# A gated-delta-rule layer: VectorE's gated product and low half queued later, and one dense quarter moved behind the solve's first products

## The chip, the cores and the metric

The kernel runs on one core of one Trainium2 chip. The metric is the device time of one execution in microseconds (us); less is better. A core has TensorE (PE: matrix products into PSUM banks), VectorE (DVE), ScalarE (ACT), GpSimd (POOL) and SyncE (SP), which issues the transfers from HBM. Each engine works through its own list of instructions in order, and waits on semaphores that the others raise.

## What is computed

Two blocks of two layers each run on a sequence of 512 tokens with 1024 features. The change lies in one of the four: the first layer of the second block, a gated delta rule (GDN) with 8 query/key heads and 16 value heads of 128 features. Cut to what matters:

```python
def gated_delta_rule(q, k, v, g, beta):          # chunks of 64 tokens
    L = jnp.where(strict, einsum('bhncd,bhnsd->bhncs', kb, k) * decay, 0.0)
    T = triangular_solve(eye + L, eye, lower=True, unit_diagonal=True)
    u = T @ vb
    w = T @ (kb * exp(g))
    ...
    def step(state, inp):
        v_new = u_n - w_n @ state
        o = q_n @ state + a_n @ v_new
        state = state * gl_n + k_n.T @ v_new
...
o = rmsnorm(o, norm_w) * silu(z)
return o.reshape(B, S, GDN_V_WIDTH) @ w_out
```

The projection before (q, k, v, z) and the one behind (`w_out`) are dense products with 1024 and 2048 rows; `T` is the inverse that the text calls the solve.

## The kernel before

All products are in fp32 precision, made of three products of high and low halves: a weight block (128 x 1024) is loaded as `w_raw`, ScalarE copies its high half (`w_hi`, L261), VectorE subtracts to get the low half (`w_lo`, L267), and PE multiplies hi by hi, hi by lo and lo by hi (L281). The same is done with the layer's output before `w_out`: `o_hi` by ScalarE (L2819), `o_lo` by VectorE (L3020).

The GDN layer works through its 8 query/key heads in 8 turns, of kinds "first" (turn 0), "mid" (turns 1 to 6) and "last" (turn 7). Turn j solves and scans head j, projects q, k, v0 and v1 of head j + 1 and z0 and z1 of its own, and multiplies the gated output of head p = j - 1 by its rows of `w_out` (output tiles `O0` to `O7`). The first turn has no p, and the last has no next head, so it projects only z0 and z1.

The order on every engine is written out by hand. On PE, `turn` alternates a small step of the solve or the scan with dense work named in the table `GDN_BESIDE`: `beside("inv")` issues the units listed at "inv", and so on. A unit such as `v02` is one dense quarter: part 2 of the projection v0, six products of 128 x 512. A unit such as `O0` is one output tile, also six products; the first one, `O0`, waits for `lo_1`, the last piece of `o_lo`.

The steps around the change, in PE's order, each followed by its dense work:

- "inv": while VectorE eliminates 16 by 16 blocks (`ta`, `tb`, 15 pairs of small instructions, then `P` and `PT`), PE has only dense quarters.
- `halves("f")` and `halves("g")` need `PT`; then the dense work of "c".
- `halves("f2")` needs `fb` (ScalarE) and `gb` (VectorE); then "f2".
- `halves("v")` needs `f2a` (ScalarE) and `f2b` (VectorE, L3096); then "v".
- `halves("y")` needs `vb` (VectorE) and `c` (ScalarE); then "y"; then `halves("at")`.

All five are issued at L2495. VectorE's order before the change, from `PT`: one `w_lo`; the convolution of the next q (`conv(0, ...)`, three instructions at L2973); `gated` (two instructions at L3015, `sq * zs`, 128 x 512); `ga` and `gb` (L3092); `ha` and `hb` (L3030); `f2b` (L3096); one `w_lo`; `low` (two instructions at L3020, which wait for `o_hi`); `va` and `vb` (L3030); one `w_lo`; and the convolutions of k and v. The last turn has the same order without the convolutions. Its dense work is `O0` beside "v" and `O1` beside "y", and nothing at "c" and "f2".

ScalarE makes `o_hi` in `high(p)`, behind its copies for `f2a` and `c`, and it waits for `gated` there.

Of the kernel before, what the change touches and what calls it, by code (L numbers as in the profile page):

```python
# [117 lines left out]
def first_and_second_block(nc, a, out):  # L118

    with ExitStack() as ctx:  # L120
# [20 lines left out]
        def tile(name, k, n=1, dt=F32):  # L141

            assert k + n <= 48
            return nc.alloc_sbuf_tensor_at(name, [P, n * T], dt, offset=arena + k * T * 4)
# [1224 lines left out]
        class Gla:  # L1369
            b0, t0 = BASE["gla"]  # L1370
            a_lr = tile("gla_a_lr", 8)
            q, k, v, g = ([gla_qkvg[:, n * T:n * T + T] for n in range(n0, n1)] for n0, n1 in ((0, 2), (2, 4), (4, 8), (8, 12)))
# [458 lines left out]
        class Dsa:  # L1831
            b0, t0 = BASE["dsa"]
            kk, wi, qi = tile("dsa_kk", 8), tile("dsa_wi", 9), [tile(f"dsa_qi{m}", 10 + m) for m in range(2)]
            q, k, v = ([dsa_qkv[:, n * T:n * T + T] for n in range(n0, n1)] for n0, n1 in ((2, 10), (0, 2), (10, 12)))
# [9 lines left out]
            p, pT = [tile(f"dsa_p{m}", 8 + m) for m in range(4)], [tile("dsa_pT0", 45), sumsq]  # L1844
# [441 lines left out]
        class Gdn:  # L2286
# [10 lines left out]
            _, inv, tmp = (gdn_blocks[:, k * P:k * P + P].rearrange("p (i c) -> p i c", i=INV_BLOCK) for k in range(3))  # L2297
# [21 lines left out]
        class GdnAt:  # L2319
# [19 lines left out]
            def through(self, n, i):  # L2339
# [4 lines left out]
        GDN_BESIDE = {  # L2344
# [60 lines left out]
        def gdn_gate(at, i, h):  # L2405

            t = at.t - 2 + h
            return (block_done, SPLIT + at.b - 1 + h + i * 16), bank[t % BANKS], (tile_free, BANKS + t + i * 28), (tile_free, BANKS + t + 1 + i * 28)
# [5 lines left out]
        def first(h):  # L2414
            return bank[(4, 7)[h]]

        def second(h):
            return bank[(5, 6)[h]]
# [505 lines left out]
        def gdn_dve(dve):  # L2924
# [18 lines left out]
            def split(at, i, n):  # L2943
                split_lo(dve, at.block[n] + AHEAD, i, 16)

            p = GDN_QK - 1
# [19 lines left out]
            def conv(u, j, i, at, odd):  # L2966
                dve.wait_ge(*at.through(GDN_CONV[u], i))
                dve.wait_ge(*N.act.after(f"cw{u}", j))
                c, src = gdn_conv(u, odd), at.bank(GDN_CONV[u])
                for d, n in ((1, "a"), (2, "b"), (3, None)):  # L2970
                    if d > 1:
                        dve.wait_ge(*N.dve.after(f"c{'ab'[d - 2]}{u}", j))
                    ins = dve.scalar_tensor_tensor(c[:, d:T], src[:, 0:T - d], par[:, gdn_tap(3 - d, u, j)], c[:, d:T], ALU.mult, ALU.add)  # L2973
                    if n:
                        ins.then_inc(*N.dve.done(f"c{n}{u}"))
                    else:
                        ins.then_inc(tile_free, 1)
# [33 lines left out]
            def gated(p, gates):  # L3011
                for h in range(2):
                    dve.wait_ge(*GdnOut.dve.after(f"on_{h}", p))
                    dve.wait_ge(*gates[h])
                    dve.tensor_tensor(G.sq[h][:], G.sq[h][:], G.zs[h][:], ALU.mult).then_inc(*GdnOut.dve.done(f"o_{h}"))  # L3015

            def low(p):
                for h in range(2):
                    dve.wait_ge(*GdnOut.act.after(f"hi_{h}", p))
                    dve.tensor_tensor(G.o_lo[h][:], G.sq[h][:], G.o_hi[h][:].bitcast(F32), ALU.subtract).then_inc(*GdnOut.dve.done(f"lo_{h}"))  # L3020

            def turn(j, p, i, at):
# [3 lines left out]
                def done(step):  # L3026
                    return H.dve.done(step)

                def tt(step, out, x, y, op):
                    dve.tensor_tensor(out, x, y, op).then_inc(*done(step))  # L3030

                def splits(point):
                    for n in GDN_LOWS[at.kind].get(point, "").split():
                        split(at, i, n)
# [44 lines left out]
                def halves(x):  # L3079
                    return x.rearrange("p (c x) -> p c x", x=INV_PART)  # L3080

                def eye(r):
                    return ident[r, r].rearrange("p (c x) -> p c x", c=1).to_broadcast([P // 2, 2 * TT, INV_PART])
                if more:
                    if p is not None:
                        dve.wait_ge(*gdn_gate(at, i, 1)[3])
                    conv(0, j + 1, i, at, odd)
                if p is not None:
                    gated(p, [gdn_gate(at, i, h)[3] for h in range(2)])
                pe("g")  # L3090
                for n, r, src in (("ga", a, second(0)), ("gb", b, second(1))):
                    dve.tensor_copy(G.m[r, :], src[r]).then_inc(*done(n))  # L3092
                for n, r, src in (("ha", a, second(0)), ("hb", b, second(1))):
                    tt(n, halves(G.V1[r, :]), halves(src[r]), eye(r), ALU.add)
                pe("f2")
                dve.tensor_copy(G.F2[b, :], first(1)[b]).then_inc(*done("f2b"))  # L3096
                splits("vc")
                if p is not None:
                    low(p)
                pe("v")  # L3100
                own("hb")
                for n, r, src in (("va", a, second(0)), ("vb", b, second(1))):
                    tt(n, G.V[r, :], G.V1[r, :], src[r], ALU.add)
                splits("f")
                if more:
                    conv(1, j + 1, i, at, odd)
# [10 lines left out]
                for t in range(TT):  # L3117
# [28 lines left out]
                    splits(f"vn{t}")  # L3146
                splits("end")
            gdn_turns(dve, turn)
            share_low(1)
            scaled_share(0)  # L3150
# [64 lines left out]
        class Fox:  # L3215
# [4 lines left out]
            q2, q3, k2, k3 = ([tile(f"fox_{n}_{h}", 8 + 2 * k + h, dt=F32R) for h in range(2)] for k, n in enumerate(("q2", "q3", "k2", "k3")))  # L3220
            q, k, v = (tile(f"fox_{n}", 16 + t) for t, n in enumerate(("q", "k", "v")))
# [3 lines left out]
            gated = tile("fox_gated", 46)  # L3225
# [557 lines left out]
        y_T, y = tile("y_T", 8, KT), tile("y", 30, KT)  # L3783
# [193 lines left out]
```

## Time and profile before

| | |
|---|---|
| median of 3 runs | 2736.06 us (2734.93 to 2736.99) |
| the profiled execution, whole time | 2736.56 us |
| its span, first to last instruction | 2734.8 us |
| granted TensorE clock, mean | 0.998 of full speed |
| PE busy | 2681.2 us (98%) |
| VectorE busy | 1787.3 us (65%) |
| ScalarE busy | 1274.7 us (47%) |
| GpSimd busy | 899.6 us (33%) |
| six mid turns of the GDN layer | from about 1928 to 2340 us, 68.7 us each |
| the last turn | from about 2335 to 2390 us |

Busy times are shares of the span. A PE that is busy 98% of it leaves few gaps, and it is the gaps on PE that a change of order can close or open. The granted clock is the share of full speed that the throttle let through.

### The profile page before, as it was taken

How to read it: one execution, taken by the hardware profiler on the slowest of the kernel's cores; microseconds unless marked ns; L12 is line 12 of the kernel's file. 1: busy time of each engine (PE TensorE's matmuls, PEld its weight loads, DVE VectorE, ACT ScalarE, POOL GpSimd, SP SyncE). 2: the span in 40 equal slices, each digit the busy share in tenths (PEclk: the TensorE clock that was granted, in tenths of full speed). 3: DMA queues.
4: the chain of work that ended last, by engine and by line, in shares of the span. 5: the costliest groups of instructions: out<-in, count | busy, mean ns of one | idle time of the engine just before them, and what ended most of it. 6: DMA issues, size and time to landing. Idle time of an engine off the chain costs nothing.

```text
span 2734.8 us, 40987 instructions
## 1 busy us (share of the span) xinstructions
PE 2681.2 (98%) x15550; PEld 2223.8 (81%) x15550; DVE 1787.3 (65%) x2641; ACT 1274.7 (47%) x2008; POOL 899.6 (33%) x751
## 2 busy tenths in 40 slices
PE   8999999999999999999999999999999999899998
PEld 6998888789888898887788998877777777777777
DVE  7974336569753687635956887348777777676664
ACT  4542232445323453223554543345555555467775
POOL 5520013136431264403733545104422222122232
PEclk9999999999999999999999999999999999999999
DMA  5343332223553325533213256322222222122222
GB/s 144 87 123 93 96 82 78 82 80 101 170 159 94 96 85 157 175 96 85 78 31 90 83 145 181 106 70 71 78 70 70 70 70 63 44 78 65 66 62 70
DMA packets 484876, 255.94 MB, mean 94 GB/s; under 512 B 17843, under 2 KB 478422, under 8 KB 484710
## 3 DMA queue, kind: packets, MB, share of 16 engines
q1 hardware_dynamic: 484534, 253.40, 32.4%
q8 instruction: 111, 1.82, 0.3%
q14 instruction: 55, 0.45, 0.1%
q10 hardware_dynamic: 176, 0.27, 0.0%
HBM read 251.51 MB, written 2.13 MB: 93 GB/s over the span
## 4 chain that ended last, share of the span: by engine, by line
PE 89%; DVE 6%; ACT 2%; issue 1%; POOL 1%; DMA 0%; SPq 0%; DVEq 0%; ACTq 0%; POOLq 0%
PE bank L281 60%; PE bank L978 12%; PE bank L2495 1%; PE bank L2526 1%; PE bank L2528 1%; DVE w_lo L267 1%; PE bank L2527 1%; DVE dsa_work L2191 1%; PE bank L3435 1%; PE bank L3427 1%; DVE small L2185 1%; PE bank L2640 1%; PE bank L3460 1%; DVE gdn_blocks L3030 1%; PE bank L1569 1%
## 5 line engine op out<-in xcount | busy, mean ns | idle before, releaser
L267 DVE TENSOR_TENSOR w_lo<-w_raw,w_hi 128x1024 fp32r<-128x1024 f32 x365 | 463.1, 1271 | 463.2 <-ACT w_hi L261 443.8
L281 PE MATMUL bank<-x_hi,w_hi 128*128 128x512 f32 x1808 | 737.7, 408 | 6.0 <-DVE w_lo L267 4.2
L281 PE MATMUL bank<-x_lo,w_hi 128*128 128x512 f32 x1808 | 707.8, 391 | 0.6 <-DVE x_lo L623 0.6
L281 PE MATMUL bank<-x_hi,w_lo 128*128 128x512 f32 x1808 | 707.5, 391 | 0.0
L261 ACT ACTIVATE w_hi<-w_raw 128x1024 fp32r<-128x1024 f32 x349 | 366.9, 1056 | 489.7 <-PE bank L281 440.7
L281 PEld LDWEIGHTS bank<-x_hi,w_hi 128*128 128x128 f32 x1808 | 340.4, 188 | 88.1 <-issue 16.5
L281 PEld LDWEIGHTS bank<-x_hi,w_lo 128*128 128x128 f32 x1808 | 340.1, 188 | 74.3
L281 PEld LDWEIGHTS bank<-x_lo,w_hi 128*128 128x128 f32 x1808 | 341.1, 189 | 68.1 <-DVE x_lo L623 3.9
L468 POOL TENSOR_TENSOR sumsq<-sumsq,sq 128x512 f32<-128x512 f32 x56 | 90.3, 1613 | 711.8 <-ACT sq L456 711.2
L281 PE MATMUL bank<-h_hi,w_hi 128*128 128x512 f32 x768 | 300.3, 391 | 0.0
L281 PE MATMUL bank<-h_hi,w_lo 128*128 128x512 f32 x768 | 299.0, 389 | 0.0
L281 PE MATMUL bank<-h_lo,w_hi 128*128 128x512 f32 x768 | 298.8, 389 | 0.0
L281 PEld LDWEIGHTS bank<-h_hi,w_hi 128*128 128x128 f32 x768 | 144.2, 188 | 30.6
L281 PEld LDWEIGHTS bank<-h_hi,w_lo 128*128 128x128 f32 x768 | 144.2, 188 | 30.5
L281 PEld LDWEIGHTS bank<-h_lo,w_hi 128*128 128x128 f32 x768 | 144.2, 188 | 29.4
L978 PE MATMUL bank<-t_hi,w_hi 128*128 128x256 f32 x512 | 146.1, 285 | 0.7 <-DVE w_lo L1192 0.7
L978 PE MATMUL bank<-t_lo,w_hi 128*128 128x256 f32 x512 | 144.8, 283 | 0.0
L978 PE MATMUL bank<-t_hi,w_lo 128*128 128x256 f32 x512 | 144.8, 283 | 0.0
L716 POOL TENSOR_TENSOR sumsq<-sumsq,ada_hi 128x512 f32<-128x512 f32 x48 | 62.1, 1293 | 160.9 <-DVE ada_hi L702 160.9
L978 PE MATMUL bank<-x_hi,w_hi 128*128 128x256 f32 x384 | 109.2, 284 | 0.3
L978 PE MATMUL bank<-x_lo,w_hi 128*128 128x256 f32 x384 | 108.7, 283 | 0.0
L978 PE MATMUL bank<-x_hi,w_lo 128*128 128x256 f32 x384 | 108.6, 283 | 0.0
(542 smaller groups left out, 5070.1 us busy)
## 6 DMA issues: line engine op xcount, KB each, us to landing
w_raw<-in_ffn_wi_dram SPq DMA_DIRECT2D x176, 512.0 KB, 3.8
w_raw<-in_ffn_wo_dram SPq DMA_DIRECT2D x64, 512.0 KB, 3.5
w_raw<-in_ada_w_dram SPq DMA_DIRECT2D x48, 512.0 KB, 4.8
w_raw<-in_a_w_in_dram SPq DMA_DIRECT2D x48, 512.0 KB, 4.0
w_raw<-in_b_w_in_dram SPq DMA_DIRECT2D x32, 512.0 KB, 4.0
w_raw<-in_ffn_wo_dram SPq DMA_DIRECT2D x32, 384.0 KB, 3.1
w_raw<-in_even_w_in_dram SPq DMA_DIRECT2D x16, 512.0 KB, 4.0
w_raw<-in_a_w_out_dram SPq DMA_DIRECT2D x16, 512.0 KB, 3.5
```

What stands on the lines that cost most here:

```text
L261: act.activation(w_hi[b % SPLIT][:], w_raw[raw % RAW][:], ACT.Copy).then_inc(w_hi_done, 1)
L267: dve.tensor_tensor(w_lo[s][:], w_raw[raw_of(b) % RAW][:], w_hi[s][:].bitcast(F32), ALU.subtract).then_inc(w_lo_done, 1)
L281: mm = pe.matmul(out, lhs[:, w], rhs(kt), start=first and kk == 0 and m == 0, stop=last and kk == len(kts) - 1 and m == 2)
L468: pool.tensor_tensor(sumsq[:], sumsq[:], sq[k % 2][:], ALU.add).then_inc(sum_added, 1)
L716: pool.tensor_tensor(dst, x, y, ALU.add).then_inc(ada_added, 1)
L978: mm = pe.matmul(out, lhs[:, w], rhs[:, k, :], start=first and k == 0 and m == 0, stop=k == 3 and m == 2, skip_group_check=True)
L1569: pe.matmul(out[:], w_hi[b % SPLIT][:, w], h_hi[:, x], start=first and kt == kts[0], stop=False)
L2185: dve.max(S.top8, w).then_inc(*s.done(f"top{t}_{k}"))
L2191: dve.match_replace(w, S.top8, w, TAKEN).then_inc(*s.done(f"out{t}_{k}"))
L2495: mm = pe.matmul(out[:, c * INV_PART:(c + 1) * INV_PART], lhs(c), rhs(c), start=True, stop=True)
L2526: pe.matmul(out[:], w_hi[s][:, x], G.o_hi[h][:], start=h == 0, stop=False)
L2527: pe.matmul(out[:], w_hi[s][:, x], G.o_lo[h][:], start=False, stop=False)
```

## The change

Two things are moved and nothing is added or taken away. In the table for mid turns, the dense quarter `v02` goes from "inv" (in front of `f` and `g`) to "c" (behind them, in front of `f2`). In VectorE's turn, of every kind that has a p, `gated` goes from in front of `ga` to behind `hb`, and `low` goes from in front of `va` to behind `vb`.

```diff
-            "mid": {... "inv": "k0 k1 k2 k3 v00 v01 v02", "c": "v03", "f2": "v10", "v": "v11 v12", "y": "v13 O0",
+            "mid": {... "inv": "k0 k1 k2 k3 v00 v01", "c": "v02 v03", "f2": "v10", "v": "v11 v12", "y": "v13 O0",
...
                     conv(0, j + 1, i, at, odd)
-                if p is not None:
-                    gated(p, [gdn_gate(at, i, h)[3] for h in range(2)])
                 pe("g")
                 for n, r, src in (("ga", a, second(0)), ("gb", b, second(1))):
                     dve.tensor_copy(G.m[r, :], src[r]).then_inc(*done(n))
                 for n, r, src in (("ha", a, second(0)), ("hb", b, second(1))):
                     tt(n, halves(G.V1[r, :]), halves(src[r]), eye(r), ALU.add)
+                if p is not None:
+                    gated(p, [gdn_gate(at, i, h)[3] for h in range(2)])
                 pe("f2")
                 dve.tensor_copy(G.F2[b, :], first(1)[b]).then_inc(*done("f2b"))
                 splits("vc")
-                if p is not None:
-                    low(p)
                 pe("v")
                 own("hb")
                 for n, r, src in (("va", a, second(0)), ("vb", b, second(1))):
                     tt(n, G.V[r, :], G.V1[r, :], src[r], ALU.add)
+                if p is not None:
+                    low(p)
                 splits("f")
```

## Rows read from the trace of the kernel before

**Rows 1.** The page: the chain that ended last, by engine.

```profile
PE 89%; DVE 6%; ACT 2%; issue 1%; POOL 1%; DMA 0%; SPq 0%; DVEq 0%; ACTq 0%; POOLq 0%
```

**Rows 2.** Busy time of each engine over six windows, one per mid turn: sum.

```profile
sum 412.00, PE 402.57 PEld 326.66 DVE 300.63 ACT 226.74 POOL 120.33; mean PE 67.10 PEld 54.44 DVE 50.11 ACT 37.79 POOL 20.06
```

**Rows 3.** PE's waits, 1890 to 2400 us: total, times, longest (us).

```profile
PE bank L2495 <- issue: 7.6, 6, 1.6
PE bank L2495 <- DVE gdn_W L3030: 1.8, 6, 0.3
```

**Rows 4.** The chain of waits in one mid turn: start, length (us).

```profile
2002.38 9.74 PE bank L281 x42
...
2014.14 1.59 PE bank L281 x6
```

**Rows 5.** PE's timeline, same turn: start, length; in brackets the idle before.

```profile
2012.06 1.15 PE L2495 MATMUL bank<-gdn_E,gdn_P 64*64 64x64 f32 x32
...
2014.07 0.50 PE L281 MATMUL bank<-x_hi,w_hi 128*128 128x512 f32 x1
...
2016.93 0.27 PE L2495 MATMUL bank<-gdn_W,gdn_W 64*64 64x64 f32 x2 [1.20 <-issue]
...
2019.61 1.15 PE L2495 MATMUL bank<-gdn_W,gdn_W 64*64 64x64 f32 x32
2020.69 0.50 PE L281 MATMUL bank<-x_hi,w_hi 128*128 128x512 f32 x1
...
2024.01 0.24 PE L2495 MATMUL bank<-gdn_W,gdn_W 64*64 64x64 f32 x1 [0.31 <-DVE gdn_W L3030]
```

**Rows 6.** VectorE's timeline in the same turn.

```profile
2010.27 0.71 DVE L3076 STREAM_TRANSPOSE gdn_P<-gdn_P 128x512 f32<-128x512 f32 x1
...
2012.01 2.31 DVE L2973 SCALAR_TENSOR_TENSOR gdn_qT<-bank,par,gdn_qT 128x511 f32<-128x511 f32 x3
2014.23 1.28 DVE L3015 TENSOR_TENSOR gdn_sq<-gdn_sq,gdn_zs 128x512 f32<-128x512 f32 x2
2015.43 1.40 DVE L3092 COPY gdn_W<-bank 64x512 f32<-64x512 f32 x2
2016.87 1.41 DVE L3030 TENSOR_TENSOR gdn_W<-bank,ident 64x512 f32<-64x512 f32 x2
2018.19 0.69 DVE L3096 COPY gdn_W<-bank 64x512 f32<-64x512 f32 x1
2018.91 1.23 DVE L267 TENSOR_TENSOR w_lo<-w_raw,w_hi 128x1024 fp32r<-128x1024 f32 x1
2021.13 1.29 DVE L3020 TENSOR_TENSOR gdn_o_lo<-gdn_sq,gdn_o_hi 128x512 fp32r<-128x512 f32 x2 [1.00 <-ACT gdn_o_hi L2819]
2022.46 1.40 DVE L3030 TENSOR_TENSOR gdn_W<-gdn_W,bank 64x512 f32<-64x512 f32 x2
```

**Rows 7.** PE's timeline in the last turn.

```profile
2358.22 0.27 PE L2495 MATMUL bank<-gdn_W,gdn_W 64*64 64x64 f32 x2 [1.55 <-DVE gdn_W L3092]
...
2360.27 1.15 PE L2495 MATMUL bank<-gdn_W,gdn_W 64*64 64x64 f32 x32 [0.89 <-DVE gdn_W L3096]
2362.58 0.47 PE L2526 MATMUL bank<-gdn_o_hi,w_hi 128*128 128x512 f32 x1 [1.16 <-issue]
...
2364.14 0.27 PE L2495 MATMUL bank<-gdn_W,gdn_W 64*64 64x64 f32 x1
```

**Rows 8.** VectorE's timeline in the last turn.

```profile
2359.48 0.69 DVE L3096 COPY gdn_W<-bank 64x512 f32<-64x512 f32 x1
2361.19 1.29 DVE L3020 TENSOR_TENSOR gdn_o_lo<-gdn_sq,gdn_o_hi 128x512 fp32r<-128x512 f32 x2 [1.02 <-ACT gdn_o_hi L2819]
```

**Rows 9.** PE's timeline in the first turn.

```profile
1885.70 1.40 PE L2495 MATMUL bank<-gdn_E,gdn_P 64*64 64x64 f32 x32 [2.15 <-DVE gdn_P L3076]
```

**Rows 10.** Busy time and PE clock, two windows, first and last turn.

```profile
1885.70:1890.00 4.30, 4.30 (x67) 3.98 (x68) 3.11 (x5) 2.24 (x3) 4.30 (x4) 0.60 0.02 4
...
2354.00:2360.00 6.00, 3.24 (x112) 3.02 (x112) 5.91 (x9) 2.81 (x4) 0.00 (x0) 1.00 0.33 90
```

2 rows, old and new, of the table GDN_BESIDE are left out of this document.

## The prediction

> **What bounds the kernel now.** I read the page first. The chain that ended last runs on PE for 89% and on VectorE for 6% [rows 1], so a change of order is worth only the PE gaps that it closes, less those that it opens. The edit touches the GDN layer alone, so I took busy time by turn next. In six mid turns, 412.00 us, PE is busy 402.57 [rows 2]: some 1.6 us of gap in a turn of 68.7. PE's waits over the layer name them [rows 3]: six gaps in front of the small products at L2495 put down to "issue", 7.6 us in all, and six for VectorE at L3030, 1.8 us. One of each falls in every mid turn, and the two timelines of one turn show which they are.
>
> The "issue" gap is that of `f2` at 2016.93 [rows 5]. The product waits for `gb`, which ends at 2015.43 + 1.40 = 2016.83, 0.10 before it [rows 6]; so the gap is a wait for VectorE, although the view does not name one. The other, 0.31, is in front of `y` at 2024.01, behind `vb`, which ends at 2022.46 + 1.40 = 2023.86. VectorE works without a pause from `PT` to the `w_lo` at 2018.91 [rows 6]. What stands between `PT` and `gb` there includes `gated`, which PE does not need until much later.
>
> **The change in a mid turn, step by step**, in the times of this turn.
>
> - `f` and `g`. They need `PT`, which ends at 2010.27 + 0.71 = 2010.98 [rows 6], and started at 2012.06, so PE now has about 1.1 us of cover. A dense quarter in that run takes 9.74 / 7 = 1.39 [rows 4]. Without `v02`, PE would be there at 2010.67, before `PT`; with 0.15 from the end of a VectorE result to the product (2023.86 to 2024.01), `f` starts at 2011.13. A wait of about 0.45 is new here.
> - "c". `f` and `g` take 2014.07 - 2012.06 = 2.01 [rows 5], so the dense work starts at 2013.14. One quarter there takes 1.59 [rows 4], a second one 1.39: 2.98. PE is ready for `f2` at 2016.12.
> - `gb`. `gated` gave VectorE 2015.43 - 2014.23 = 1.20 of work in front of it. Now `ga` starts at 2014.23 (`g` is over by about 2013.3), and `gb` ends at 2014.23 + 1.40 = 2015.63. This is before 2016.12: the gap of 1.20 is closed, and `f2` starts 0.81 earlier.
> - `f2b`. The same instructions stand before it, `gated` now behind `hb`, so it still ends at 2018.19 + 0.69 = 2018.88. `f2` and the quarter behind it take 2019.61 - 2016.93 = 2.68, and PE is ready for `v` at 2018.80. With 0.10 of delay `v` starts at 2018.98: a wait of 0.18 is new, and `v` is 0.63 earlier than before. VectorE, not PE, now sets this point.
> - `y`. `v` takes 2020.69 - 2019.61 = 1.08, two quarters 2.98: PE is ready at 2018.98 + 4.06 = 2023.04. The results of `v` reach VectorE at about 2018.98 + 1.2 = 2020.2; the `w_lo` is done at 2020.14, and `va` and `vb` follow without `low` in front: `vb` ends at 2021.6. The gap of 0.31 is closed. `y` starts 0.97 earlier.
> - `low`. It runs from 2021.6 to 2022.9; even the `o_hi` of before was there by 2021.13 [rows 6]. `gated`, which `o_hi` waits for, ends at 2018.2 instead of 2015.5, still 2.9 in front of that, so I count nothing for it. `O0` reads `lo_1` behind `y` and one quarter, at 2023.04 + 1.08 + 1.59 = 2025.7, with 2.8 us in hand; if that cover were gone, each microsecond would count in full.
> - The rest. From `vb` on VectorE is about 1.1 ahead of its old times, PE 0.97. The `w_lo` pieces, the convolutions and the chain of the scan follow the one or the other, and so does GpSimd, which waits for `vb`. Block v0 ends some 0.4 later than before on PE, long before ScalarE and VectorE convolve it. No transfer is moved: SP's order is untouched, and its loads wait for `w_lo` pieces which come no later.
>
> Six mid turns: 6 x 0.97 = 5.8 us gained. A lower bound is 0.63 per turn (3.8), if the second gap does not close.
>
> **The first turn** has no p, and its table is not changed: nothing.
>
> **The last turn** has no convolution and little dense work, and takes the same order on VectorE. Before it, `ga` followed `g` almost at once, with `gated` hidden in the wait for `g`; so `f2`, at 2358.22 behind `gb` [rows 7], gains nothing. `gated` now delays `f2b` by 1.20: its end goes from 2359.48 + 0.69 = 2360.17 [rows 8] to 2361.37, and `v` starts at 2361.47. The results of `v` come at 2362.67, `va` and `vb` take 1.40 to 2364.07, and then `low` takes 1.29 to about 2365.3. But `O0`, the dense work beside "v", waits for `lo_1`: before, it started at 2362.58, 0.10 behind `low` [rows 7, 8]. Now it starts at 2365.4, with `va`, `vb` and `low` all in front of it and PE idle, and `y` stands behind `O0` on PE. `y` and all that follows are 2.8 us later; nothing in this turn can give it back, as what follows is a chain paced by PE and by its own results.
>
> **The clock.** PE would be idle from about 2359.4 to 2365.4 but for 1.15 us of `v`. In the first turn, after an idle of 2.15 us [rows 9], the granted clock fell shortly after the small products began, and the 4.30 us behind were run at a mean of 0.60 [rows 10]: its lower level, 1.2 GHz, for most of it. That is 4.30 x 0.40 = 1.7 us of work at full speed lost. In the last turn of before, PE was busy 3.24 of 6.00 us and the clock stayed at 1.00 [rows 10]. Now the pauses are 2.1 and 2.8 us, so a fall is likely. Its price lies between nothing (it falls and is released inside the pause) and 1.7; I take 1.3, nearer the upper end, since the dense work starts directly behind the pause.
>
> The Trainium skill (TensorE: Matmul & The Clock Gate, "What's actually happening") has it that half rate is the default and that activity releases it. By that rule the work behind the pauses starts at half rate; by the last turn of before alone it would stay at full speed, and the kernel would be 1.3 us faster than I forecast. The trace agrees with the rule in the first turn, with the 0.60 above.
>
> **The sum.** -5.8 + 2.8 + 1.3 = -1.7 us. The profiled execution took 2736.56 us (span 2734.8 and 1.8 around it), 0.5 above the median of the runs, so I take the difference alone to the median: 2736.06 - 1.7 = 2734.4 us.
>
> **The rivals.**
>
> - The clock holds in the last turn: -5.8 + 2.8 = -3.0, 2733.1 us. For it: it held there before. Against it: [rows 9, 10]. Chance 0.22.
> - The mid turns don't keep their gain: some other chain (ScalarE's roots, VectorE's elimination in the next turn) is the true pace, and only the last turn's loss is seen: +2.8 + 1.3 = +4.1, 2740.2 us, slower. Its place is the new wait in front of `f`: if it grows until it eats the gain. For it: VectorE is the last to come at `f` and at `v` after the change. Against it: from PE's sums of one turn to the elimination of the next, VectorE's work starts from PE's own result, so it moves with PE, and I have counted that wait (0.45). It decides the sign where the gain of a turn is below 4.1 / 6 = 0.68. Chance 0.1, of which 0.04 for a loss over 0.2%.
> - The last turn loses nothing, as `low` and `O0` find cover that I don't see: -5.8, 2730.3 us. Against it: `O0` waits for `lo_1` already now. Chance 0.06.
> - The change does nothing, both edits cancelling in every turn: 2736 us. It would need `f` to wait 1.4 rather than 0.45. Chance 0.04.
>
> My forecast has 0.58.
>
> **How the numbers follow.** A change of 0.2%, 5.5 us, is about what a measurement of this kernel can tell from none. My forecast, the clock's rival and most of the second one lie inside. Beyond -5.5 lies only the rival of the last turn, at its edge: faster 0.05. Beyond +5.5 only a second rival with a further loss: slower 0.04. The range runs from 2731.2, the upper bound of the gain with part of the last turn's loss, to 2737.6, the lower bound of the gain (3.8), 2.8 and a clock fallen in full (1.7), which is +0.7, and the spread of the runs of before (1 us either way).
>
> **What the changed profile would show.** In a mid turn: `f2` with no gap in front, a gap of 0.4 to 0.5 in front of `f` and one of about 0.2 in front of `v` released by L3096, none in front of `y`; six windows of 67.7 us instead of 68.7. In the last turn: `v` 1.2 later behind `f2`, a pause of about 2.8 in front of `O0`, and a granted clock under 1.00 around it. I am wrong if mid turns stay at 68.7, or if `O0` starts right behind `v` there.

## The result and the profile after

The changed kernel takes 2746.77 us (median of 6 runs, 2745.87 to 2748.40) against 2736.30 us of the kernel before (6 runs): a ratio of 1.0039, 95% interval 1.0027 to 1.0051. It is 10.5 us slower. I had forecast 2734.4, 1.7 us faster, and given a loss of over 0.2% a chance of 0.04.

The profiled execution took 2745.87 us, with a span of 2744.1 (before 2734.8), 9.3 us longer. The start of `PT` (L3076) in each turn divides it. From turn 1 to turn 7 it is 2357.5 - 1939.6 = 417.9 us, against 2353.7 - 1941.6 = 412.1: six mid turns of 69.65 us instead of 68.68, +5.8. From `PT` of the last turn to the copy of T (L3109) it is 19.9 us against 14.3: +5.6. From the first turn's `PT` to turn 1 it is 55.3 against 56.8, and `PT` of the first turn came 0.5 earlier: together 2.0 us less, which has nothing to do with the edit. In the profiled execution of before the granted clock fell in the first turn [rows 9, 10], and in this one it did not; over all profiled executions of this study that stretch takes 56.7 or 56.8 us where the clock falls in it and 55.3 where it does not. What follows the copy of T is 0.1 shorter: 5.8 + 5.6 - 2.0 - 0.1 = 9.3. Through the six mid turns the granted clock is 1.00 in both executions, so their 5.8 us are not the clock's.

PE's waits over the mid turns of the changed kernel (us in total, times, longest):

```profile
PE bank L2635 <- DVE gdn_W L3141: 5.1, 6, 0.9
PE bank L2495 <- DVE gdn_P L3076: 2.6, 6, 0.8
PE bank L2495 <- issue: 2.3, 6, 0.4
PE bank L2526 <- DVE gdn_kT L2973: 1.8, 6, 0.3
PE bank L2640 <- ACT gdn_T L2826: 1.2, 6, 0.2
```

They answer to [rows 3]. The gaps in front of `f2` (7.6) and `y` (1.8) are gone, and the waits that I had foreseen are there: `f` behind L3076, 0.4 a turn, and `v`, 0.4 ("issue"). Three more are new, all behind VectorE's work after `vb`: an output tile waits for the convolution of k, the scan for `ct` (a copy by ScalarE, which had itself waited for that convolution), and the first product of the scan's second step (L2635) 0.9 us for VectorE's copy of the state.

VectorE's timeline of one mid turn from `ga` on, in the changed kernel, which answers to [rows 6]:

```profile
2083.05 1.40 DVE L3090 COPY gdn_W<-bank 64x512 f32<-64x512 f32 x2
2084.47 1.41 DVE L3030 TENSOR_TENSOR gdn_W<-bank,ident 64x512 f32<-64x512 f32 x2
2085.91 1.29 DVE L3015 TENSOR_TENSOR gdn_sq<-gdn_sq,gdn_zs 128x512 f32<-128x512 f32 x2
2087.24 0.69 DVE L3096 COPY gdn_W<-bank 64x512 f32<-64x512 f32 x1
2087.96 1.23 DVE L267 TENSOR_TENSOR w_lo<-w_raw,w_hi 128x1024 fp32r<-128x1024 f32 x1
2089.22 1.41 DVE L3030 TENSOR_TENSOR gdn_W<-gdn_W,bank 64x512 f32<-64x512 f32 x2
2090.66 0.69 DVE L3020 TENSOR_TENSOR gdn_o_lo<-gdn_sq,gdn_o_hi 128x512 fp32r<-128x512 f32 x1
...
2091.26 1.77 DVE L3020 TENSOR_TENSOR gdn_o_lo<-gdn_sq,gdn_o_hi 128x512 fp32r<-128x512 f32 x1
2092.96 2.31 DVE L267 TENSOR_TENSOR w_lo<-w_raw,w_hi 128x1024 fp32r<-128x1024 f32 x1
2095.30 2.32 DVE L2973 SCALAR_TENSOR_TENSOR gdn_kT<-bank,par,gdn_kT 128x511 f32<-128x511 f32 x3
```

Down to `vb` it is as forecast. Then the second piece of `low` takes 1.77 us instead of 0.69, and the `w_lo` behind it 2.31 instead of 1.23, with the same shapes: 2.2 us in which VectorE is busy by the profile and late for everything behind. GpSimd's timeline of the same stretch, in the changed kernel; `da` (L3171) and `db` (L3174), two instructions each, make the decay matrices of the next head from inputs in SBUF:

```profile
2090.70 1.78 POOL L3171 TENSOR_TENSOR gdn_dec<-gdn_gb,not_above 128x512 f32<-128x512 f32 x1 [24.54 <-DVE gdn_W L3030]
...
2092.45 1.73 POOL L3171 TENSOR_TENSOR gdn_dec<-gdn_gb,not_above 128x512 f32<-128x512 f32 x1
2094.15 2.02 POOL L3174 TENSOR_TENSOR gdn_dec<-gdn_dec,gdn_cols 128x512 f32<-128x512 f32 x1
```

GpSimd waits for `vb` and starts `da` at 2090.70, 0.04 behind the first piece of `low`. From there the two engines take turns. `low`'s second piece ends 0.55 behind the end of the first `da` (2092.48), the `w_lo` 1.1 behind the end of the second `da` (2094.18), 0.14 less than each takes alone, and each GpSimd instruction is in turn longer by what VectorE does first. In the kernel before, GpSimd started with the `w_lo` at 2023.89, and this is its row:

```profile
2023.94 2.32 POOL L3171 TENSOR_TENSOR gdn_dec<-gdn_gb,not_above 128x512 f32<-128x512 f32 x1 [26.57 <-DVE gdn_W L3030]
```

There GpSimd paid (2.32 us), and VectorE did not (1.23): it was 0.05 ahead, and the convolutions that followed, which take one input from PSUM, ran at their usual 2.31 beside `da` and `db`. The edit put `low`, two instructions with both inputs in SBUF, between `vb` and the `w_lo`. Only the first instruction of such a run has the lead.

The last turn of the changed kernel, on PE (answers to [rows 7]), and the clock of a stretch of it:

```profile
2362.03 0.27 PE L2495 MATMUL bank<-gdn_W,gdn_W 64*64 64x64 f32 x2 [1.55 <-DVE gdn_W L3090]
2365.52 1.97 PE L2495 MATMUL bank<-gdn_W,gdn_W 64*64 64x64 f32 x32 [2.33 <-DVE gdn_W L3096]
2370.35 0.77 PE L2526 MATMUL bank<-gdn_o_hi,w_hi 128*128 128x512 f32 x1 [2.86 <-issue]
```

```profile
2364.00:2373.00 9.00, 4.62 (x38) 3.63 (x38) 5.18 (x8) 2.42 (x4) 0.00 (x0) 0.50 0.02 4
```

The two pauses, 2.33 and 2.86 us, are where the prediction had them, and the granted clock is 0.50, its lower level of 1.2 GHz, for the 9 us of this window. It fell inside the first pause, at 2363.7; `v` took 1.97 us instead of 1.15 [rows 7].

### The profile page after: what moved, and what is told of

It reads as the page before. It is cut to its first block, busy times and chain, and to the rows that moved or that the text cites. A ratio compares the mean times of both kernels' runs of the same rounds, so it can differ in the third digit from the quotient of the medians.

```text
span 2744.1 us, 40987 instructions
## 1 busy us (share of the span) xinstructions
PE 2683.8 (98%) x15550; PEld 2224.5 (81%) x15550; DVE 1803.4 (66%) x2641; ACT 1274.8 (46%) x2008; POOL 904.4 (33%) x751
## 3 DMA queue, kind: packets, MB, share of 16 engines
q8 instruction: 111, 1.82, 0.3%
## 4 chain that ended last, share of the span: by engine, by line
PE 84%; DVE 12%; issue 2%; ACT 1%; POOL 1%; DMA 0%; DVEq 0%; SPq 0%; ACTq 0%; POOLq 0%
PE bank L281 57%; PE bank L978 12%; DVE w_lo L267 2%; DVE gdn_blocks L3030 2%; PE bank L2495 1%; DVE gdn_vT L2973 1%; DVE dsa_work L2191 1%; DVE small L2185 1%; PE bank L3435 1%; PE bank L3427 1%; PE bank L2526 1%; PE bank L3460 1%; PE bank L2528 1%; PE bank L1569 1%; PE bank L2527 1%
## 5 line engine op out<-in xcount | busy, mean ns | idle before, releaser
L267 DVE TENSOR_TENSOR w_lo<-w_raw,w_hi 128x1024 fp32r<-128x1024 f32 x365 | 472.2, 1298 | 461.1 <-ACT w_hi L261 441.9
```

The lines of the kernel that those rows point to most:

```text
L267: dve.tensor_tensor(w_lo[s][:], w_raw[raw_of(b) % RAW][:], w_hi[s][:].bitcast(F32), ALU.subtract).then_inc(w_lo_done, 1)
```

## The experiments

The port theory, formed from these rows: a VectorE instruction with both inputs in SBUF and a GpSimd instruction can't run at once, so `low` and the `w_lo` wait for `da`. Rivals: the moved quarter and its waits in front of `f` and `v` cost the time; or the new order costs it by itself, without GpSimd. All ratios are to runs of the kernel before on the same chip.

**GpSimd later, all else as changed** (`dve` is GpSimd's wait for a step of VectorE; `s0_1`, a step of the scan, comes some 14 us behind `vb`).

```diff
-                    dve("PT" if p is None else "vb")
+                    dve("PT" if p is None else "s0_1")
                     front(j + 1, 1 - gdn_odd(at))
```

> The changed kernel in full, but GpSimd begins its work for the next head (the decay rows, da and db) behind s0_1 instead of behind vb. Port theory: VectorE's two pieces of o_lo and the w_lo behind them are held up in the changed kernel by GpSimd's da and db, which start with them; with GpSimd out of the way they take 1.3 and 1.2 us again instead of 2.4 and 2.3, a mid turn takes 67.9 us, and the kernel is 0 to 2 us slower than before (six turns at -0.8, last turn at +5.5). Rival (the moved quarter or the order itself costs the time, not GpSimd): mid turns stay at 69.7 and the kernel stays 10 us slower.

Measured: 2736.55 us, ratio 1.0004 (0.9995 to 1.0013). All pieces of `low` are short again (least, median and longest, ns; before them the changed kernel's row):

```profile
L3020 DVE TENSOR_TENSOR gdn_o_lo<-gdn_sq,gdn_o_hi x14: 684/694/1776, 1951.2 to 2369.6; 128x512 fp32r<-128x512 f32 x14
```

```profile
L3020 DVE TENSOR_TENSOR gdn_o_lo<-gdn_sq,gdn_o_hi x14: 682/688/692, 1951.0 to 2358.8; 128x512 fp32r<-128x512 f32 x14
```

`w_lo` is at 1.21, and six mid turns take 2346.8 - 1939.4 = 407.4, 67.90 each. The order on VectorE and PE is that of the changed kernel; so the loss in the mid turns is GpSimd's overlap, and both rivals fall.

**GpSimd alone, in the kernel before.**

```diff
-                    dve("PT" if p is None else "vb")
+                    dve("PT" if p is None else "s0_1")
```

> The kernel before with GpSimd's da and db behind s0_1, nothing else. Port theory: in the old order only the w_lo behind vb runs beside them, and it was not held up (1.23 us), so a mid turn stays at 68.7 and there is no difference. Rival (GpSimd's place gains by itself, and the run with the full change and GpSimd later was fast for that): 0.8 us per turn less.

Measured: 2736.79 us, 1.0002 (0.9993 to 1.0011), mid turns at 68.70. The place of GpSimd's work is worth nothing until something of VectorE's collides with it.

**GpSimd earlier, in the kernel before.**

```diff
-                    dve("PT" if p is None else "vb")
+                    dve("PT" if p is None else "hb")
```

> The kernel before with one edit: GpSimd begins da and db behind hb instead of behind vb, so that they run beside f2b, the w_lo and o_lo, in the old order on both engines. Port theory: the w_lo behind f2b and the o_lo pieces go from 1.23 and 1.29 us to above 2, vb and y come 1 to 2 us later, and the kernel is 5 to 12 us slower. Rival (only the order of the change costs): no difference.

Measured: 2749.63 us (5 runs), 1.0053 (1.0039 to 1.0067), a mid turn at 71.15: 13 us slower, a little over the upper end expected. Not all of that is GpSimd's overlap. The wait in front of `y` goes from 0.31 to 1.75 us, and in four of the six mid turns the granted clock falls soon behind it. Here is a mid turn without the fall, the next one, with it, and the stretch of the fall:

```profile
2012.34:2082.57 70.23, 67.27 (x566) 54.56 (x565) 52.21 (x95) 37.80 (x61) 20.95 (x17) 1.00 0.24 68
2082.57:2154.37 71.80, 68.84 (x566) 55.70 (x565) 52.31 (x95) 37.90 (x61) 20.95 (x17) 0.98 0.23 67
2099.40:2102.70 3.30, 3.30 (x9) 2.60 (x8) 3.16 (x6) 2.07 (x5) 0.00 (x0) 0.50 0.61 159
```

The overlap costs 1.5 us of a turn (70.2 against 68.7), some 9 us in six, which is within what was expected; the half clock costs another 1.5 in a turn in which it falls. VectorE's timeline of the second of these turns, ahead of the fall at 2099.4:

```profile
2090.49 0.69 DVE L3096 COPY gdn_W<-bank 64x512 f32<-64x512 f32 x1
2091.21 1.82 DVE L267 TENSOR_TENSOR w_lo<-w_raw,w_hi 128x1024 fp32r<-128x1024 f32 x1
2093.44 2.74 DVE L3020 TENSOR_TENSOR gdn_o_lo<-gdn_sq,gdn_o_hi 128x512 fp32r<-128x512 f32 x2 [0.41 <-ACT gdn_o_hi L2819]
2096.21 1.40 DVE L3030 TENSOR_TENSOR gdn_W<-gdn_W,bank 64x512 f32<-64x512 f32 x2
```

The same two kinds are held up, `w_lo` 1.82 for 1.23 and `low` 2.74 for 1.29, while `f2b` (one input, from PSUM) and `va` with `vb` (one of two inputs from PSUM) take what they always take, although GpSimd runs beside `f2b` and `va` too. So it is neither the place in the order nor GpSimd's being busy as such, but the operands.

**The quarter alone** (the table as changed, VectorE as before).

```diff
-            "mid": {... "inv": "k0 k1 k2 k3 v00 v01 v02", "c": "v03", ...
+            "mid": {... "inv": "k0 k1 k2 k3 v00 v01", "c": "v02 v03", ...
```

> Only the table is changed: v02 behind g in mid turns, VectorE's order as before. Port theory and the sum of the prediction: f comes 0.9 earlier, but f2 still waits for gb, so nothing moves: a mid turn at 68.7, no difference. Rival (the moved quarter is the cost): mid turns near 69.7, 6 us slower.

Measured: 2736.80 us, 0.9999 (0.9990 to 1.0008), mid turns at 68.70. `f` waits 0.38 behind `PT`, and the wait in front of `f2` shrinks from 1.20 to 0.78 by about as much. The quarter only moves PE's wait.

**The order alone, in mid turns.**

```diff
-                if p is not None:
+                if p is not None and more:      # behind hb; in front of ga where not more
                     gated(p, ...)
...
-                if p is not None:
+                if p is not None and more:      # behind vb; in front of va where not more
                     low(p)
```

> VectorE's new order in full (gated and low later) in mid turns alone; the quarter v02 stays in front of f, and the last turn is as before. Port theory: the o_lo pieces and the w_lo behind them are at 2.4 and 2.3 us as in the changed kernel, a mid turn takes 69.5 to 69.8, 5 to 6 us slower. Rival (the moved quarter costs): mid turns at 68 to 68.7, same or faster.

Measured: 2742.18 us, 1.0022 (1.0013 to 1.0031), mid turns at 69.65, as in the changed kernel: `low`'s longest piece is 1775 ns.

**The quarter and `gated` in mid turns, `low` left in front of `va`.** The edit is the table above and the first half of the one before.

> Only the quarter v02 and the gated product are moved, in mid turns alone; low stays in front of va, and the last turn is as before. Port theory: nothing new runs beside GpSimd, so a mid turn takes 67.9 us and the kernel is 4 to 5 us faster than before. Rival (the new waits in front of f and v are the cost): mid turns at 69.7 or near it, 6 us slower.

Measured: 2731.86 us, 0.9984 (0.9975 to 0.9993), mid turns at 67.93, `low` at 693 ns at most. This is most of the gain that I had forecast (0.75 of 0.97 in a turn), with GpSimd still behind `vb`: the lead of 0.05 then falls to the `w_lo` again.

**The new order in the last turn alone.** The conditions of the order experiment turned round (`not more`).

> VectorE's new order in the last turn alone, all else as before. From the changed kernel's trace: 5.5 us slower, with a granted clock of 0.50 around the wait in front of O0. By the prediction's terms (2.8 and 1.3) it would be 4.1.

Measured: 2741.38 us, 1.0016 (1.0007 to 1.0025): 4.1 us slower by the medians. In its profiled execution `PT` to the copy of T takes 19.9 us (before 14.3), with the clock at 0.51 from 2360 to 2370.

**The same with the pauses filled.** Products that nobody reads keep PE busy in front of `v` and of `O0`.

```diff
+                if at.kind == "last":
+                    pe.wait_ge(*at.free("O0", i))
+                    unread_products(pe, at.bank("O0"), 16)
                 act("f2a")
...
+                if at.kind == "last":
+                    unread_products(pe, at.bank("O0"), 20)
                 beside("v")
```

> As the run with the new order in the last turn alone, with products that nobody reads (16 in front of v, 20 in front of O0, 128 x 128, 0.11 us each) so that PE stays busy through the two pauses. If the half clock is part of the last turn's cost, the clock stays at 1.00 there and the loss falls from 5.5 to about 3.0 to 3.5 us, the queueing alone; if the clock costs nothing, it stays at 5.5.

Measured: 2742.48 us, 1.0018 (1.0009 to 1.0027), no better. The clock stayed at 1.00, but I had taken the price of a product from records that count two for each: 16 of them took 3.84 us instead of 1.8, so `v` and `O0` came behind the fill. This run says nothing on what the half clock costs, and I repeated it with 9 and 11.

> As the filled last turn, with 9 and 11 unread products instead of 16 and 20: the larger fill was overdone, since one product of 128 x 128 took 0.23 us, not 0.11, so that v and O0 came behind it and not behind their waits. With 2.1 and 2.6 us of fill PE is busy and late for nothing. Theory (half clock is part of the cost): clock 1.00, and from PT to the copy of T 17.2 to 17.6 us, against 14.3 before and 19.9 with the new order unfilled; 3 us slower than before. Rival (the clock costs nothing): 19.9, and no better than unfilled.

Measured: 2739.26 us, 1.0011 (1.0002 to 1.0020), 2.9 us slower than before. Its PE, and the clock from 2354 to 2370:

```profile
2357.81 2.27 PE L348 MATMUL bank<-ones 128*128 128x128 f32 x18
2360.22 1.15 PE L2495 MATMUL bank<-gdn_W,gdn_W 64*64 64x64 f32 x32
2361.30 2.72 PE L348 MATMUL bank<-ones 128*128 128x128 f32 x22
2364.23 0.47 PE L2526 MATMUL bank<-gdn_o_hi,w_hi 128*128 128x512 f32 x1 [0.21 <-issue]
```

```profile
2354.00:2370.00 16.00, 14.11 (x239) 12.28 (x235) 8.95 (x14) 8.03 (x13) 0.00 (x0) 1.00 0.25 67
```

`PT` to the copy of T is 17.5 us. `O0` starts 12.0 us behind `PT`, against 8.8 in the kernel before: 3.2, all queueing. So of the 5.6 us that the last turn loses in the trace, 3.2 are the queueing and 2.4 the half clock. This split rests on one profiled execution of each kernel; by the medians the fill brings back 1.2 us (2.9 lost instead of 4.1, on different chips), and the intervals overlap.

**`gated` alone, in the last turn.**

> Only gated is moved, in the last turn alone; low stays in front of va. f2b is 1.3 us later and v with it; low runs in the wait for v, and O0 is no later than v allows, so the loss is 1.3 us and at most 1 us more for a granted clock that falls: 1 to 2.5 us slower in the trace. The rest of the last turn's 5.5 is then low in front of O0 and its clock. Rival (gated is all of it): 4 or more.

Measured: 2739.53 us, 1.0011 (1.0002 to 1.0020), and 17.2 us from `PT` to the copy of T: +2.9, more than the 2.5 expected. The queue costs what was said: `f2b` is 1.3 later, `low` runs in the wait for `v`, and `O0` follows `v` at once. But the clock fell inside the pause of 2.33 us in front of `v`, and `v`, `O0` and most of `y` ran at half of it. `low` adds the rest.

**The whole change in mid turns, GpSimd later, the last turn as before.**

> The whole change in mid turns, the last turn as before, and GpSimd behind s0_1. If the two causes (the shared port in mid turns, low in front of O0 in the last) are all there is, it is 4 to 5 us faster than before, with mid turns at 67.9. If something else is in it, it is slower than that.

Measured: 2732.11 us, 0.9982 (0.9973 to 0.9991), mid turns at 67.92. With both causes out, what is left is most of the forecast gain (5.2 of 5.8 us).

**`gated` later still.** As the last one, with `gated` behind `f2b` and its `w_lo` in mid turns.

```diff
                 dve.tensor_copy(G.F2[b, :], first(1)[b]).then_inc(*done("f2b"))
                 splits("vc")
+                if p is not None and more:
+                    gated(p, [gdn_gate(at, i, h)[3] for h in range(2)])
```

> Toward a faster version: in mid turns the quarter behind g, gated behind f2b and its w_lo, low behind vb, GpSimd behind s0_1; the last turn as before. f2b no longer has gated in front, so the wait in front of v (0.38 us) closes: a mid turn of 67.5 to 67.6 instead of 67.9, and 6 to 7 us faster than before. Rival (o_hi comes too late for low, or low for O0): 67.9 or more.

Measured: 2730.16 us, 0.9976 (0.9966 to 0.9985): 6.2 us faster than before, by the medians the best kernel of this study (the intervals of the last run and of the quarter with `gated` overlap its own). PE's only named wait in its mid turns is the one for `PT`:

```profile
PE bank L2495 <- DVE gdn_P L3076: 2.6, 6, 0.8
```

A mid turn takes 67.53.

## Why the prediction was wrong, point by point

- **`f`, `f2`, `v`, `y`.** Right, within 0.2 us. `f` waited 0.38 (0.45 forecast), `f2` did not wait, `v` waited 0.38 (0.18), `y` did not. The difference at `v` is that `gated` takes 0.23 us more behind `hb` than it did in front of `ga`: 2087.24 - 2083.05 = 4.19 from `ga` to `f2b`, against 1.20 + 2.76 = 3.96. By the rows, `gated` and the instruction behind it started 0.08 to 0.09 us before the end of the one ahead in the old place, and start 0.03 to 0.04 behind it in the new one. The gain kept over a turn is 0.78 (68.68 to 67.90), not 0.97.
- **"The rest", in the mid turns.** This is the step that failed: "From `vb` on VectorE is about 1.1 ahead of its old times." Two instructions behind `vb` took 2.2 us more, and a turn lost 0.97 instead of gaining it. I had moved `low` next to GpSimd's start, named that start ("GpSimd, which waits for `vb`"), and costed `low` at the 1.29 of [rows 6], where nothing ran beside it. (By the step's own times the lead is 0.97, 2023.86 to 2022.89, and not "about 1.1"; nothing hangs on that.) The runs with GpSimd moved settle it: later, the loss goes; earlier, it comes back in the old order. Six turns: +5.8 where the sum had -5.8; that the two are equal in size is chance.
- **The last turn.** The mechanism was right: `low` in front of `O0`, PE idle, the clock fallen. The queueing was 3.2 (2.8 forecast) and the clock 2.4 (1.3, with 1.7 as its upper bound). The bound was too low because the clock stayed at half not for one stretch of 4 us, as in the first turn, but for the 9 us of the window shown, through `v`, the pause and `O0`. By medians the turn costs 4.1 us and not 5.6. A part of the difference is that the old order is not free of the clock either, which I had read from one execution ("the clock stayed at 1.00"): of the eight profiled executions with the old last turn the clock fell in four, and the turn took 14.8 to 15.8 us in these and 14.3 in the others, 0.5 more on average. The rest of the difference, about 1 us, is not explained.
- **The rivals.** The second one had the right sign for a wrong cause, "the new wait in front of `f`": that wait stayed at 0.38. No rival named a price that changes with what runs beside an instruction. The range's upper end was built from gains that shrink, never from one that turns (its terms, 2736.06 + 0.7 + 1, give 2737.8 and not 2737.6, which changes nothing).
- **The parts add up.** Order in mid turns +5.6, last turn +4.1, quarter 0: 9.7, for 10.5 measured, each by medians on its own chip.

The Trainium skill has the rule that I did not weigh (SBUF — State Buffer, "Who interferes with whom"): a VectorE instruction with two SBUF inputs contends with a GpSimd instruction that reads SBUF, one with at most one SBUF input, outside the 2-port perf modes, does not, and "issue order, not op shape, decides who blocks". The traces agree: 1.77 against 0.69 us for `low`, 2.31 against 1.23 for `w_lo`, no change for the convolutions, and the lead of 0.04 to 0.05 us decides who pays.

That the instructions share a port is the word of the Trainium skill; what the runs show is that these kinds of instructions exclude each other, and which. Why `gated` starts later behind `hb` was not tried.

## What to carry to other kernels

Before moving an instruction on VectorE, read GpSimd's timeline at the place that it goes to, and what starts GpSimd there. An instruction's duration is that of its place: where two engines exclude each other and a semaphore starts both, the one that is ahead by a few hundredths of a microsecond runs free and all that follow it alternate, so keep one such instruction there, not three, or start the other engine in a stretch whose instructions read PSUM. And follow an order shared by loops into the turn with the least dense work: what hides a step in six turns was missing in the seventh.

## What the runs showed of the hardware that I had not expected

- VectorE and GpSimd alternated instruction by instruction. In one mid turn of the changed kernel VectorE lost 2.2 us, while `da` and `db` took 6.5 us (3.48 + 3.02) instead of the 4.6 (2.52 + 2.04) of the run with GpSimd later. The profile counts the time on both sides as busy.
- In all four profiled executions with a pause of 2.33 us on PE in front of `v`, behind one of 1.55 (changed, GpSimd later, last turn alone, `gated` alone), the clock fell to half inside that pause. It stayed there, through little work, for over 9 us in the first three and some 7 in the fourth (a mean of 0.66 from 2360 to 2370). With the pauses in front of `v` and `O0` filled it did not fall in this turn, in either execution. In the old order, with pauses of 1.55, 0.89 and up to 1.16, it fell in four executions of eight, and came back sooner: one trace in which the clock holds does not show that it will hold in the next.
